# First input projection of a two-layer block: feature rows as the outer loop, modulation summed in pairs

## What is computed

```python
c_act = silu(c)
for l in range(2):
    mod = c_act @ w_ada[l] + b_ada[l]                    # 1024 -> 3 x 1024
    shift, scale, gate = jnp.split(mod, 3, axis=-1)
    h = rms_norm(x, g_pre[l]) * (1.0 + scale) + shift
    proj = h @ w_in[l]                                   # 1024 -> 3072 = six groups of 512
    y_a = b_a * causal_depthwise_conv(c_a * u_a, w_conv[l]) * silu(gate_a)
    y_p = causal_multiscale_pool(u_p, w_pool[l], pool_scale[l]) * silu(gate_p)
    y = jnp.concatenate([y_a, y_p], axis=-1) @ w_out[l]
    x = x + gate * rms_norm(y, g_post[l])
```

## Time and profile before

| what | value |
|---|---|
| three runs | 1283.46, 1284.05, 1284.75 us (median 1284.05) |
| profiled execution, its own time | 1283.19 us |
| its span on the core | 1281.5 us |
| PE, DVE, ACT, POOL busy | 97%, 69%, 50%, 13% of the span |
| TensorE's granted clock over the span | 0.993 |
| the chain that ended last, by engine | PE 86%, DVE 6%, DMA 4%, ACT 2%, POOL 1%, issue 1% |
| loads of 1 MB, issue to landing, median | 5.0 to 6.0 us by kind |

### The profile page before, as it was taken

One profiled execution on the slowest core, in us unless ns is written; L12 is line 12 of the kernel. 1 busy time (PEld: TensorE's weight loads), 2 busy tenths in 40 slices (PEclk: granted clock), 3 DMA queues, 4 the chain that ended last, 5 costly groups with the idle time before them and its releaser, 6 DMA issues.

```text
span 1281.5 us, 19572 instructions
## 1 busy us (share of the span) xinstructions
PE 1247.1 (97%) x7756; PEld 1110.4 (87%) x7756; DVE 887.6 (69%) x931; ACT 641.2 (50%) x825; POOL 172.2 (13%) x217
## 2 busy tenths in 40 slices
PE   3999999999999999989999999999999999999998
PEld 2899899888888899978988888888889998988887
DVE  6769666676666767987766667666667687766665
ACT  2445545554444456855544444444446676644442
POOL 8400100088200110000100001000001221200000
PEclk9999899999999999999999999999999999999999
DMA  9897495455556362324555554665554444456551
GB/s 364 267 315 270 160 328 179 149 194 184 186 191 196 117 220 66 128 71 131 182 183 194 195 183 147 229 197 187 180 191 160 148 153 151 151 192 196 196 196 66
DMA packets 167104, 236.88 MB, mean 185 GB/s; under 512 B 5172, under 2 KB 146624, under 8 KB 164992
## 3 DMA queue, kind: packets, MB, share of 16 engines
q1 hardware_dynamic: 165920, 234.57, 54.8%
q0 software_dynamic: 816, 0.89, 0.3%
q10 hardware_dynamic: 304, 0.53, 0.1%
HBM read 234.92 MB, written 1.05 MB: 184 GB/s over the span
## 4 chain that ended last, share of the span: by engine, by line
PE 86%; DVE 6%; DMA 4%; ACT 2%; POOL 1%; issue 1%; DVEq 0%; ACTq 0%; POOLq 0%
PE acc L2191 23%; PE acc L2193 12%; PE acc L2227 5%; PE acc L2228 5%; PE acc L2229 5%; PE acc L2209 4%; PE acc L2210 3%; PE acc L2211 3%; DVE wlo L1355 2%; DMA raw<-in_w_in_dram 2%; PE acc L2599 2%; PE acc L2245 2%; PE acc L2128 2%; DVE region L1362 1%; PE acc L2129 1%; PE acc L2130 1%
## 5 line engine op out<-in xcount | busy, mean ns | idle before, releaser
L1355 DVE TENSOR_TENSOR wlo<-raw,whi 128x2048 fp32r<-128x2048 f32 (+1 forms) x199 | 453.8, 2283 | 200.1 <-ACT whi L746 199.2
L746 ACT ACTIVATE whi<-raw 128x2048 fp32r<-128x2048 f32 (+1 forms) x199 | 378.1, 1904 | 183.5 <-PE acc L2229 113.1
L2191 PE MATMUL acc<-hT,whi 128*128 128x512 f32 x1280 | 320.2, 392 | 0.5 <-ACTq L827 0.5
L2191 PEld LDWEIGHTS acc<-hT,whi 128*128 128x128 f32 x1280 | 232.4, 189 | 43.9 <-issue 0.7
L2193 PEld LDWEIGHTS acc<-hT,wlo 128*128 128x128 f32 x1280 | 174.6, 190 | 12.5
L2193 PE MATMUL acc<-hT,wlo 128*128 128x256 f32 x1280 | 178.5, 282 | 0.0
L2227 PE MATMUL acc<-whi,sT_hi 128*128 128x512 f32 x320 | 125.0, 391 | 0.0
L2228 PE MATMUL acc<-wlo,sT_hi 128*128 128x512 f32 x320 | 125.0, 390 | 0.0
L2229 PE MATMUL acc<-whi,sT_lo 128*128 128x512 f32 x320 | 124.5, 389 | 0.0
L2209 PE MATMUL acc<-whi,hT 128*128 128x256 f32 x416 | 120.2, 289 | 1.1 <-DVE hT L1429 1.1
L2210 PE MATMUL acc<-wlo,hT 128*128 128x256 f32 x416 | 117.6, 283 | 0.0
(11 more groups left out here) (324 smaller groups left out, 1952.2 us busy)
## 6 DMA issues: line engine op xcount, KB each, us to landing
raw<-in_ffn_w_in_dram SPq DMA_DIRECT2D x88, 1024.0 KB, 5.1
raw<-in_ffn_w_out_dram SPq DMA_DIRECT2D x44, 1024.0 KB, 5.0
raw<-in_w_ada_dram SPq DMA_DIRECT2D x24, 1024.0 KB, 5.6
raw<-in_w_in_dram SPq DMA_DIRECT2D x24, 1024.0 KB, 6.0
raw<-in_diff_w_in_dram SPq DMA_DIRECT2D x12, 1024.0 KB, 5.2
raw<-in_nsa_w_in_dram SPq DMA_DIRECT2D x10, 1024.0 KB, 5.3
raw<-in_w_out_dram SPq DMA_DIRECT2D x8, 1024.0 KB, 5.0
raw<-in_nsa_cmp_w_dram SPq DMA_DIRECT2D x4, 1024.0 KB, 5.5
```

The costliest lines, as they stand in the source:

```text
L746: nc.scalar.activation(whi[:, w % SPL, 0:n], raw[:, r % RAW, 0:n], ACT.Copy).then_inc(hi_ready, 1)
L1355: nc.vector.tensor_tensor(wlo[:, w % SPL, 0:n], raw[:, r % RAW, 0:n], whi_f[:, w % SPL, 0:n], ALU.subtract).then_inc(raw_done, 1)
L2191: nc.tensor.matmul(o, hi[:, kt, cs], hT[:, :, kt, :], start=kt == 0, stop=False)
```

## The change

Only the stages up to the end of layer 0 are rewritten.

- The shift and scale columns of `w_ada[0]` no longer pass through `raw`. They are loaded as eight half pairs, each half of the 1024 rows by 256 shift and 256 scale columns (two DMAs), into a ring of three buffers that lies in `proj`. `add_pair` sums one with four operations on 512 columns. After two halves TensorE sums over partitions (`sum_pair`), and two of the eight feature tiles have their shift and gain (`pair_modulation`, L1662 to L1665).
- The first half of the projection (the pooled columns and both gates: columns 1536 to 3071) is read as eight row items of 128 x 1536, one per feature tile. Six PSUM banks accumulate at once; TensorE works through one feature tile after the other (`row_high`, `row_low`, `row_last`). Four banks are zeroed first by matmuls of zeros (`clear_gates`).
- x is loaded first. The transposed x is kept in `xT`; ACT applies shift and gain per pair, DVE takes the low parts (`features`, `features_lo`).
- The other six column chunks follow (`COLS1`), with two side items behind each from the second on. All sixteen side and out items keep their content.
- Of the small parameters only `b_ada` and `g_pre` are loaded early, on ACT's queue; the others move on POOL behind the statistics, and the small weights wait for all eight rows.
- `keep_clock` shrinks from five matmuls to one.

```diff
-    items = [("ada", 0, kt) for kt in range(KD)]
-    side = [("gate", 0, c) for c in range(4)] + [("ada", 1, kt) for kt in range(KD)]
...
+    items = [("w", "row", kt) for kt in range(KD)]
+    cols = [("w", "in1", 0, c) for c, _ in COLS1]
...
+    items += cols[0:2] + gate[0:2] + cols[2:3] + gate[2:4] + cols[3:4] + ada[0:2] + cols[4:5] + ada[2:4] + cols[5:6]
+    items += ada[4:6] + outs[0:1] + ada[6:7] + outs[1:2] + ada[7:8] + outs[2:4]
...
+PAIRS_AHEAD = {0: 2, 1: 2, 2: 1, 3: 1, 4: 1, 5: 1}
...
+            def load_pair(i):
+                f, half = i // 2, i % 2
+                if i >= PAIR_RING:
+                    sp.wait_ge(pair_done, i - PAIR_RING + 1)
+                rows_v = a["w_ada"][0][half * 512:(half + 1) * 512, :].rearrange("(k p) n -> p k n", p=P)
+                for s in range(2):
+                    sp.dma_start(pair_raw[:, i % PAIR_RING, :, s, :], rows_v[:, :, s * D + f * CC:s * D + (f + 1) * CC])\
+                      .then_inc(pair_landed[i % PAIR_RING], 16)
...
+            add_pair(0, 0)
+            add_pair(0, 1)
+            row_lo(1)
+            pair_modulation(0)
+            add_pair(1, 0)
+            features_lo(0)
+            add_pair(1, 1)
+            row_lo(1)
+            pair_modulation(1)
...
+            def sum_pair(f):
+                pe.wait_ge(pair_sums, f + 1)
+                for j in range(4):
+                    ins = nc.tensor.matmul(acc[:, 6, 4 * f + j:4 * f + j + 1],
+                                           acc_pair[:, f % 2, j // 2, (j % 2) * P:(j % 2 + 1) * P], ones[:, 0:1],
+                                           start=True, stop=True)
+                ins.then_inc(pair_ps, 1)
...
+            row_high(0, False)
+            row_high(0, True)
+            row_low(0)
+            row_high(1, False)
+            row_high(1, True)
+            sum_pair(1)
+            row_low(1)
```

More of the change, by code:

```diff
@@ L384, in size @@
         def size(item):
+            if item[1] == "row":
+                return ROWN
             return 8 * NGATE if item[1:] == ("nsa", 10) else CH
@@ L462, in _ @@
                 else:
[L463 removed]
+                    if r == 0:
                         sp.dma_start(x[:, :, :], a["x"][0].rearrange("(t p) n -> p t n", p=P)).then_inc(x_landed, 16)
+                    for _ in range(PAIRS_AHEAD.get(r, 0)):
+                        load_pair(n_pair)
+                        n_pair += 1
                     load(r)
@@ new lines, in features @@
+            def features(f):
+                act.wait_ge(pair_ready, f + 1)
+                if f == 0:
+                    act.wait_ge(xT_ready, 2)
+                    act.wait_ge(xT0_ready, 2)
+                if f > 1:
+                    act.wait_ge(feat_ready, 2 * (f - 1))
+                for k in range(2):
+                    kt = 2 * f + k
+                    step(nc.scalar.activation(h_pair[:, f % 2, k, :], xT[:, kt, :], ACT.Identity,
+                                              bias=shift1[:, 0, kt:kt + 1], scale=gain1[:, 0, kt:kt + 1]))
+                    nc.scalar.activation(hT_hi[:, kt, :], h_pair[:, f % 2, k, :], ACT.Copy).then_inc(feat_hi, 1)
@@ new lines, in _ @@
+            split_to(0)
+            features(0)
+            split_to(1)
+            features(1)
+            split_to(2)
+            split_to(3)
+            features(2)
+            split_to(4)
+            split_to(5)
+            features(3)
+            b0 = w_at[("in1", 0, COLS1[0][0])]
+            split_to(b0)
+            act.wait_ge(rows_done, 1)
+            nc.scalar.activation(p0[:, :, :], acc[:, 4:6, :], ACT.Copy).then_inc(proj_ready, 2)
+            split_to(b0 + 1)
+            for c, b in ROW_GATES:
+                evict_row_gates(c, b)
@@ new lines, in features_lo @@
+            def features_lo(f):
+                for k in range(2):
+                    kt = 2 * f + k
+                    dve.wait_ge(feat_hi, kt + 1)
+                    nc.vector.tensor_tensor(hT_lo[:, kt, :], h_pair[:, f % 2, k, :], hT_hi_f[:, kt, :],
+                                            ALU.subtract).then_inc(feat_ready, 1)
+            dve.wait_ge(consts_ready, 1)
+            step(nc.vector.reciprocal(pos1[:, :], pos1[:, :]))
+            for g, w in enumerate(WINDOWS):
+                step(nc.vector.tensor_scalar(count_fix[:, g, :], pos1[:, :], float(w), 1.0, ALU.mult, ALU.max))
@@ L1605, in _ @@
                         modulation(l, 1)
[L1606 to L1613 removed]
+                        convolve(l)
                     if n == 10:
@@ new lines, in sum_pair, with row_high @@
+            def sum_pair(f):
[5 more added lines that the diff above has]
+                ins.then_inc(pair_ps, 1)
+            def row_high(kt, low):
+                w = w_at[("row", kt)]
+                hi = whi[:, w % SPL, 0:ROWN]
+                src = hT_lo if low else hT_hi
+                if low:
+                    pe.wait_ge(feat_ready, kt + 1)
+                else:
+                    pe.wait_ge(feat_hi, kt + 1)
+                    pe.wait_ge(hi_ready, w + 1)
+                for tt in range(TT):
+                    nc.tensor.matmul(acc[:, 4 + tt, :], src[:, kt, tt * P:(tt + 1) * P], hi[:, CW:2 * CW],
+                                     start=kt == 0 and not low, stop=False)
+                for c, b in ROW_GATES:
+                    for ft in range(2):
+                        at = (c - 6) * CC + ft * P
+                        nc.tensor.matmul(acc[:, b, ft * T:(ft + 1) * T], hi[:, at:at + P], src[:, kt, :],
+                                         start=False, stop=False)
```

528 lines of the change are left out of this document (355 added, 173 removed).

## The result

The changed kernel took 1296.47 us (median of four runs, 1296.38 to 1303.99), beside 1284.4 us for the kernel before in the same session (1283.46 to 1284.94). The ratio is 1.0101, with a 95% interval of 1.0073 to 1.013: slower, by about 1%. The medians are 12.1 us apart; in the profiled executions 1296.38 stands against 1283.19, so +13.2 us.

A forecast was written before the change was run, and what follows sets the result against it. The three-slot `raw` ring, with TensorE just behind, was taken to bound layer 0. The last out chunk at 144.5 against 133.1 and TensorE's end at 148.8 against 136.0 gave +12.7 on 1283.19: 1295.9, forecast 1296, range 1287 to 1307.

The forecast's parts named there:

- Start and prices: Head of the kernel: vector engine starts pairs at 14.6 us; sums cost 0.49 and 0.79, a pair 6.0, low part 1.67.
- Waits of the rows' stage: Vector engine's added waits on TensorE and the scalar engine until the rows' low parts end at 65.9: 8.3 us, bounds 0 and 20.
- the half clock at the first parts: TensorE's first row parts, normally 1.42 us: two priced at 2.85 and one at 1.9, putting pair 1's sum at 34.8.
- The ring: Column chunks behind the rows: load, high part and low part in series, 10.1 us a period, 3.4 an item.
- Which limit ends last: Behind the rows: serial slot time sets the pace; side items hide inside it except before chunk 5 and out chunk 1.
- The end: Layer 0's end: TensorE gets out chunk 2 at 141.8 and finishes at 148.8, against 136.0 before.
- Rival 1: TensorE's earlier start survives because loads and chunks arrive as wanted: 4.4 us faster, 1278.8; chance 0.06.
- Rival 2: Rows' stage: the 8.3 us of waits vanish, since TensorE and the scalar engine are early: +4.4, 1287.6; chance 0.14.
- Rival 3: TensorE at half clock after gaps, four rows at the low level: 1303 to 1308, 7 us more at worst; chance 0.15.
- Rival 4: Pair loads in 1 KB pieces take longer and starve the sums: 1 us more each, 1300 to 1304; chance 0.05.
- The load's fixed share: Ring's 1 MB load: trace's 5.1 to 5.9 us used; the skill's 4.4 would make the sum an estimated +6.
- +12.7: Forecast slowdown in us: TensorE's end of layer 0 at 148.8 against 136.0, with everything later shifted equally.

The follow-up runs named there:

- both edits: Changed kernel with high and low parts in halves and layer 0's side sums cut to 64 columns behind the first row tile: 1290.13 us, ratio 1.002.

## Why the prediction came out right

The time (1296 forecast, 1296.47 measured), the direction and the end of layer 0 (148.8 forecast, 148.84 measured) hold. By its steps:

- **Start and prices.** Pairs start at 13.95 (14.6 forecast). The sums cost 0.48 and 0.79 us (0.49 and 0.79), a pair 6.0, a row's low part 1.76 or 1.71 in pairs (1.67). Prices read along a line through three sizes of the old trace carried over to 512 columns. (TensorE's start at 24.4 is 23.95 by its own terms; its first row came at 23.66.)
- **Waits of the rows' stage: right place, wrong split.** I had 8.3 us: 3.8 at pair 1, 1.1 at the last pair's sum, 3.4 behind it. Measured are 3.8 in three nearly equal waits at the three sums and 2.6 behind the last (1.18, 0.51, 0.95). The failed step is the half clock at the first parts: I priced two at the low and one at a rising clock, but only the first part ran slow (23.66 to 26.33 us), and TensorE reached the sum at 32.0, not 34.8. What I priced once comes at every pair: a wait of 0.97, 1.36 and 1.43 us. Moving the sum ended all three, and the period fell to 10.6. The second of them was the clock's, by the execution that kept 1.00 there and had no wait. Rows' low parts ended at 64.5 (65.9 forecast).
- **The ring: right sum from two wrong terms, by luck.** I took 10.1 us for each period, with a load of 5.86 that I read as one with nothing ahead of it; in fact the side load before it was under way until 47.67. Periods were 9.5 with loads of 5.0 to 5.2 us, and 12.3 for the one load that met the small weights (7.96). I had priced the moved small loads at nothing, with the pooled product as the only one to wait for them; that they are under way together with the chunk on the path was missing, and costs some 1.5 us by the run with them earlier. The start of the ring's part was 1.4 us earlier than forecast, too (62.86 against 64.3). That the too long and the too short terms cancel to 0.04 us at the mark is chance.
- **Which limit ends last.** I counted the side sums as hidden except at chunk 5 and out chunk 1. The trace agrees up to 101 us. From there on the vector engine's list is the limit with the loads directly under it, and it took both edits to gain 6.3 us (5.1 by the mark). "Idle several us in every period from 75 to 140" was wrong for TensorE: 2.1 us of idle time lie between 66 and 101, 10.6 between 101 and 144. It still had the rows' backlog in the first part. The vector engine idled 15.9 us between 66 and 144 (over 10 forecast).
- **The end.** TensorE got out chunk 2 at 141.77 (141.8) and was done at 148.8. What lies behind moved by 0.5 us more.
- **Rival 1** (the head start survives) falls: TensorE's first half ended at 69.9 us, 5.6 us ahead by my count (4.4 forecast). It was still 2.5 us ahead at the tenth part (101.9 us) and 2.2 at the eleventh, and 5.8 behind at the twelfth (123.4 us).
- **Rival 2** (waits vanish) did not happen by itself, and was within reach: its price of 8.3 was too high, since the waits measured are 6.4 us, and removing what order could remove gave 5.5 us at the mark and 4.3 in the time.
- **Rival 3** (half clock). It did happen on a small scale. Low stretches came, 0.50 to 0.70 in six windows of 3 or 4 us. Behind 75 us they were worth about half a microsecond, by the run that filled three of the gaps. In the rows' stage the one of 36 to 40 us (0.57) cost 1.4 us, by the execution without it. What the first one (21 to 27 us) cost stays open.
- **Rival 4** (slow pairs): the vector engine had no wait on a half pair's load; all its waits there are on TensorE and the scalar engine.
- **The load's fixed share.** By the Trainium skill (DMA: Bandwidth & Descriptors, Anatomy of one DMA), whose fit is for transfers issued by GpSimd, a load would take an estimated 4.4 us and the sum be +6. The shortest loads in the chain of the changed kernel, issued by SyncE, took 5.03 to 5.20 us, so the measurement decides, and +12.7 was the better sum.

## What to carry to other kernels

A ring of three slots gives a period of load plus split plus release to every third item, 9.5 us here. If a reorder puts the items that an engine waits for three apart instead of two, look at that serial time, even where every engine has idle time; but count by items too, since here the ring was no slower than before and only had more left to load. When an edit that clearly shortens a link moves nothing, look for a second limit right under it and relieve both in one run before you drop the edit. And after a reorder, read each wait on a strictly ordered queue for the work that stands behind it: such swaps, with the halves of two copies, side items moved, the small weights earlier and no work removed, gave back all of the loss here. And before you credit an edit with a microsecond of one profile, compare the granted clock of the stretches ahead of it.

## What the runs showed of the hardware

- The loads of 1 MB in the changed kernel's chain behind 62 us were never alone, and took 5.0 to 8.0 us. The ones issued at 84.65 and 94.14 us took 5.20 and 5.03, with a side load issued earlier under way for 0.8 and 0.7 us more and others issued 2.5 and 1.2 us after them. The one at 72.33 took 7.96: a side load issued at 67.81 was under way until 77.14, and the last of 0.75 MB of small weights until 75.80. The rule is not that simple, though: 6.44 us (small weights earlier) and 6.27 us (113.81) came with only 0.7 to 0.8 us left of the load ahead.
- TensorE's granted clock stood at 0.50 (its 1.2 GHz level) at 21 to 24 us after a start with gaps, and was back at 1.00 in 27 to 30 us. It fell again to 0.57 in 36 to 40 us, where TensorE had just stood 2.5 us for a high part, and to 0.64 at 136 to 140 us after a gap of 3.6 us. It is not the same in every execution: behind the same gap of 2.53 us it stayed at 1.00 in one, and 1.4 us were saved. With products of 128 columns in the gaps it stood at 1.00 from 112 to 116 and from 136 to 140 us.
- Splitting a copy of 2048 columns in two costs little: 1.92 us on the scalar engine became 1.06 twice, started 1.09 apart, and 2.30 on the vector engine became 1.23 twice, started 1.26 apart.
